# Two junctions of a two-block transformer kernel: second output projection reordered, gate/up token sums made from PSUM

## The reference

```python
mixed = jnp.concatenate([rms_norm_2(attn, attn_out_norm[l]),
                         rms_norm_2(sgu, sgu_out_norm[l])], axis=-1)
y = mixed @ w_out[l]                                   # second output projection
x = x + rms_norm_2(y, post_mix_norm[l])
h = rms_norm_2(x, pre_ffn_norm[l])
f = (jax.nn.silu(h @ w_gate[l]) * (h @ w_up[l])) @ w_down[l]
x = x + rms_norm_2(f, post_ffn_norm[l])
```

## Time and profile before

| | |
|---|---|
| median of 3 runs | 2080.42 us (2078.24 to 2081.92) |
| the profiled execution | 2081.29 us, its span 2079.5 us |
| TensorE busy | 2004.0 us, 96% of the span, 10021 matmuls |
| VectorE, ScalarE, GpSimd busy | 1325.6, 846.2, 960.3 us (64%, 41%, 46%) |
| mean granted TensorE clock | 0.987 of full speed |
| chain that ended last | TensorE 79%, VectorE 11%, ScalarE 5%, GpSimd 2% |

### The profile page before, as it was taken

The page is one execution under the profiler, slowest core; times in us unless marked ns, Lnnn a source line. Parts: engine busy times, 40 slices in busy tenths (PEclk is TensorE's granted clock), DMA queues, the critical chain, the costliest instruction groups (busy, mean ns, idle before and its releaser), DMA issues.

```text
span 2079.5 us, 27399 instructions
## 1 busy us (share of the span) xinstructions
PE 2004.0 (96%) x10021; PEld 1662.3 (80%) x10021; DVE 1325.6 (64%) x1744; ACT 846.2 (41%) x1349; POOL 960.3 (46%) x564
## 2 busy tenths in 40 slices
PE   7999999999999999999999899897999999999997
PEld 6888888888887778878887689775788888878885
DVE  7887777756637655874331543799665656657977
ACT  5444544434420034560202676566333332334443
POOL 1344555332233477733542200848755555435552
PEclk8999999999999999999999999999999999999998
DMA  9223212211122143242111000231333323346344
GB/s 282 69 81 112 100 53 95 85 30 41 41 62 62 61 172 112 102 142 63 50 40 59 23 1 1 71 116 58 120 107 106 111 90 102 120 171 229 101 140 150
DMA packets 178925, 193.98 MB, mean 93 GB/s; under 512 B 9799, under 2 KB 122904, under 8 KB 178842
## 3 DMA queue, kind: packets, MB, share of 16 engines
q1 hardware_dynamic: 172420, 178.53, 26.9%
q10 hardware_dynamic: 6422, 14.37, 1.9%
HBM read 151.71 MB, written 41.16 MB: 93 GB/s over the span
## 4 chain that ended last, share of the span: by engine, by line
PE 79%; DVE 11%; ACT 5%; issue 3%; POOL 2%; ACTq 0%; DMA 0%; SPq 0%; DVEq 0%; POOLq 0%
PE psum L994 6%; PE psum L996 6%; PE psum L995 6%; PE psum L1533 6%; PE psum L1534 6%; PE psum L1535 6%; PE psum L1155 3%; PE psum L1632 3%; PE psum L1634 3%; PE psum L1633 3%; PE psum L1015 3%; PE psum L1016 3%; PE psum L1014 3%; PE psum L1436 3%; PE psum L1310 2%
## 5 line engine op out<-in xcount | busy, mean ns | idle before, releaser
L777 POOL TENSOR_TENSOR w_hi<-w_raw,ones 128x1024 fp32r<-128x1024 f32 x60 | 149.3, 2489 | 480.9 <-PE psum L996 356.7
L994 PE MATMUL psum<-h_hi,w_hi 128*128 128x512 f32 x704 | 284.1, 404 | 0.0
L996 PE MATMUL psum<-h_hi,w_lo 128*128 128x512 f32 x704 | 274.7, 390 | 0.0
L995 PE MATMUL psum<-h_lo,w_hi 128*128 128x512 f32 x704 | 274.2, 390 | 0.0
L1664 ACT ACTIVATE arena<-psum 128x1024 f32<-128x1024 f32 (+7 forms) x134 | 100.3, 752 | 215.6 <-PE psum L996 134.0
L780 POOL TENSOR_TENSOR w_lo<-w_raw,w_hi 128x1024 fp32r<-128x1024 f32 x60 | 167.9, 2799 | 4.7
L995 PEld LDWEIGHTS psum<-h_lo,w_hi 128*128 128x128 f32 x704 | 132.4, 188 | 28.4 <-issue 2.6
L994 PEld LDWEIGHTS psum<-h_hi,w_hi 128*128 128x128 f32 x704 | 132.3, 188 | 28.4 <-issue 2.6
L996 PEld LDWEIGHTS psum<-h_hi,w_lo 128*128 128x128 f32 x704 | 132.1, 188 | 28.5
L1632 PE MATMUL psum<-w_hi,h_hi 128*128 128x512 f32 x308 | 122.0, 396 | 8.1 <-DVE h_lo L3220 5.1
L1633 PE MATMUL psum<-w_lo,h_hi 128*128 128x512 f32 x308 | 121.5, 394 | 0.0
(11 more groups left out here) (483 smaller groups left out, 5315.6 us busy)
## 6 DMA issues: line engine op xcount, KB each, us to landing
w_raw<-w_in SPq DMA_DIRECT2D x64, 512.0 KB, 3.8
act_op<-arena SPq DMA_DIRECT2D x77, 256.0 KB, 2.2
arena<-act_op SPq DMA_DIRECT2D x77, 256.0 KB, 2.7
w_raw<-w_gate SPq DMA_DIRECT2D x22, 512.0 KB, 4.0
w_raw<-w_up SPq DMA_DIRECT2D x22, 512.0 KB, 5.1
arena<-ada_w SPq DMA_DIRECT2D x16, 512.0 KB, 7.2
arena<-w_out SPq DMA_DIRECT2D x16, 512.0 KB, 6.0
out_T<-arena SPq DMA_DIRECT2D x16, 512.0 KB, 5.6
```

What stands on the lines that cost most here:

```text
L994: pe.matmul(o, wh, xh, start=(k == 0), stop=False)
L995: pe.matmul(o, wh, xl, start=False, stop=False)
L996: return pe.matmul(o, wl, xh, start=False, stop=(k == KT - 1))
```

## The change

**In the projection.** GpSimd makes S1 right behind the low parts of P7 (n == 7) and T4 behind those of n == 11. VectorE takes the last attention block (`attended`) after the first low part of P1, normalises before the last one, and lays copies 1 and 3 between the low parts of steps 4 to 7; the four S2 sums come behind step 7's. ScalarE loads the table for Sqrt before its last attention copies, rounds P7's right operands before the norm, and makes copies 0 and 2 inside the loop, behind the roundings for n = 5 and n = 7; the high parts of steps 4 to 7 wait for step 0 alone. TensorE does transposes 2 and 3 one tile earlier in step 3.

**At the junction.** ScalarE makes `r12` only, three passes for each strip. VectorE makes T1, T3 and T2 of a strip as scalar-tensor-tensor operations that read B12 or B22 from PSUM. T3 is now B22 - B12, and S3 is A11 - A21 for every pair, so that their product is unchanged. All 16 low parts of the T sums are made by VectorE. GpSimd makes `whole` 0 to 3 ahead of pair 1's weight sums, then only weights. TensorE transposes the first three token tiles of B12 and B22 before the fourth is normalised (now by ScalarE), does transposes k + 2 behind the products of strip k, and the order of pair 1 is A11, A12, S4, S1, S3, S2, A22. ScalarE's table load, Silu and roundings lie between the strips.

```diff
-SECOND_PRODUCTS = ["A11", "A12", "S4", "S2", "S1", "S3", "A22"]
+SECOND_PRODUCTS = ["A11", "A12", "S4", "S1", "S3", "S2", "A22"]
...
                 if n == 7:
                     for i in range(QJ):
+                        q_sum("S1", i)
+                if n == 11:
+                    for i in range(QJ):
                         q_sum("T4", i)
-                    for i in range(QJ):
-                        q_sum("S1", i)
...
-            t_lo(0, "T2", t2_raw)
-            t_lo(1, "T1", r11)
+            second_lo("S1")
+            second_lo("S3")
             second_lo("S2")
-            second_lo("S1")
-            t_lo(2, "T3", r22)
-            second_lo("S3")
             second_lo("A22")
-            t_lo(3, "T4", r21)
...
-                        if (n, t) == (3, 3):
+                        if (n, t) == (3, 2):
                             pe.wait_ge(*raw_ready(0))
                             q_transpose(2)
...
             pe.wait_ge(o_sums, Q_C0 + Q_C11[3])
+            pe.wait_ge(xn_done, 3 * NT - 1)
+            b_transpose(0, range(3))
+            b_transpose(1, range(3))
             pe.wait_ge(xn_done, 3 * NT)
-            b_transpose(0)
-            b_transpose(1)
+            b_transpose(0, [3])
+            b_transpose(1, [3])
...
-                    act.wait_ge(o_step, Q_STEP + n - 3)
+                    act.wait_ge(o_step, Q_STEP + (n - 3 if n >= 8 else 1))
...
-            for j in range(QJ):
-                q_hi_b(QJ + j, "P7", j)
-            q_raw_copy(0)
-            q_raw_copy(2)
             for n in Q_ORDER_A[4:]:
                 q_hi_a(n, O_PRODUCTS[n // QJ], n % QJ)
                 if n < 24:
                     q_hi_b(n + 4, O_PRODUCTS[n // QJ + 1], n % QJ)
+                if n in (5, 7):
+                    q_raw_copy(n - 5)
...
-            q_raw_copy(1)
-            q_raw_copy(3)
+            q_lo(3, "P1", 3)
             dve.wait_ge(row_in, 48)
             for n in Q_ORDER_A[4:]:
                 q_lo(n, O_PRODUCTS[n // QJ], n % QJ)
-                if 4 <= n < 8:
-                    q_s2(n - 4)
+                if n in (4, 6):
+                    q_raw_copy(n // 2 * 2 - 3)
+                if n == 7:
+                    for j in range(QJ):
+                        q_s2(j)
...
+                STT(r11[:, k, :], b12, mul(k), r11[:, k, :], ALU.mult, ALU.subtract).then_inc(t_sum, 1)
+                STT(r22[:, k, :], b22_, mul(k + 4), r12[:, k, :], ALU.mult, ALU.subtract).then_inc(t_sum, 1)
+                dve.wait_ge(t_sum, 3 * k + 1)
+                STT(t2_raw[:, k, :], b22_, mul(k + 4), r11[:, k, :], ALU.mult, ALU.subtract).then_inc(t_sum, 1)
...
+            t_lo("T1", r11, lambda k: 3 * k + 3)
+            t_lo("T3", r22, lambda k: 3 * k + 3)
             dve.wait_ge(gp_done, NPR)
             dve.wait_ge(silu_b_done, 1)
             TT(act_lo, psum[:, P_BANK["u2"], :], u2_of[0], ALU.mult).then_inc(act_b_done, 1)
-            for k in range(2, 4):
-                dve.wait_ge(t_sum, 2 * k + 2)
+            dve.wait_ge(s0_done, S0_BASE + KT)
+            for k in range(4):
                 TT(r21[:, k, :], t2_raw[:, k, :], r21[:, k, :], ALU.subtract).then_inc(t_sum, 1)
+            t_lo("T2", t2_raw, lambda k: 3 * k + 3)
+            t_lo("T4", r21, lambda k: 12 + k + 1)
```

More of the change, by code:

```diff
@@ L937, in _ @@
             TT(s_raw["S4"], A12, s_raw["S2"], ALU.subtract).then_inc(s_done_w, 1)
[L938 to L957 removed]
+            TT(s_raw["S3"], A11, A21, ALU.subtract).then_inc(s_done_w, 1)
             for name in ("A11", "A12", "S4"):
@@ L2111, in _ @@
                 if n == N - 1:
+                    A(lb_tmp, ones[:, 0:8], ACT.Sqrt)
                     q_raw_copy(4)
@@ L2117, in _ @@
                 q_hi_a(j, "P1", j)
-            A(lb_tmp, ones[:, 0:8], ACT.Sqrt)
+            for j in range(QJ):
+                q_hi_b(QJ + j, "P7", j)
             act.wait_ge(ao_done, 2 * NT)
@@ L2209, in _, with b_taken, t_hi @@
             q_root(5)
-            for name in ("A11", "A12", "S4"):
-                second_hi(name)
+            second_hi("A11")
+            q_xn(5, 3, 2)
             act.wait_ge(spilled_a, 16 * 4)
             act.wait_ge(spilled_b, 16 * 2)
-            for k in range(4):
+            def b_taken(k):
                 act.wait_ge(tr_full, T_BASE[4] + KT + 2 * k + 2)
-                for e, (name, raw) in enumerate((("B12", r12), ("B22", r22))):
+                for e, name in enumerate(("B12", "B22")):
                     src = psum[:, 4 + (2 * k + e) % 4, :]
                     A(x_hi[name][:, k, :], src, ACT.Identity, scale=mul(k + 4 * e)).then_inc(b22_taken, 1)
-                    A(raw[:, k, :], src, ACT.Identity, scale=mul(k + 4 * e)).then_inc(b22_taken, 1)
+                    if name == "B12":
+                        A(r12[:, k, :], src, ACT.Identity, scale=mul(k)).then_inc(b22_taken, 1)
+            def t_hi(k):
+                for a, (name, raw) in enumerate((("T1", r11), ("T3", r22), ("T2", t2_raw))):
+                    act.wait_ge(t_sum, 3 * k + a + 1)
+                    copy(x_hi[name][:, k, :], raw[:, k, :]).then_inc(t_rounded, 1)
+            b_taken(0)
+            b_taken(1)
+            second_hi("A12")
             act.wait_ge(gp_done, 1)
             A(silu_of[0], psum[:, P_BANK["g1"], :], ACT.Silu).then_inc(silu_a_done, 1)
-            for a, name, raw in ((2, "T2", t2_raw), (1, "T1", r11)):
-                for k in range(4):
-                    act.wait_ge(t_sum, 2 * k + a)
-                    copy(x_hi[name][:, k, :], raw[:, k, :]).then_inc(t_rounded, 1)
+            second_hi("S4")
+            b_taken(2)
+            t_hi(0)
+            b_taken(3)
+            for k in range(1, 4):
+                t_hi(k)
             act.wait_ge(spilled[1], 16 * 2)
@@ L2229, in _ @@
             act.wait_ge(gp_done, NPR)
-            second_hi("S2")
-            second_hi("S1")
-            for k in range(4):
-                act.wait_ge(t_sum, 8 + k + 1)
-                copy(x_hi["T3"][:, k, :], r22[:, k, :]).then_inc(t_rounded, 1)
-            second_hi("S3")
-            second_hi("A22")
+            for name in ("S1", "S3", "S2", "A22"):
+                second_hi(name)
             for k in range(4):
@@ L2293, in _ @@
             each = [[name] for name in PRODUCTS]
-            gu_pair(1, 1, SECOND_PRODUCTS, [["A11"], [], [], ["S2"], ["S1"], ["S3"], ["A22", "A12", "S4"]], False)
+            gu_pair(1, 1, SECOND_PRODUCTS, [["A11"], [], [], [], [], ["S2", "S1", "S3"], ["A22", "A12", "S4"]], False)
             with act.Fori(1, FT // 2 - 1) as j:
@@ L3009, in _ @@
             q_raw_copy(7)
-            for j in range(QJ):
+            q_lo(0, "P1", 0)
+            attended(2 * NT - 1)
+            for j in range(1, 3):
                 q_lo(j, "P1", j)
-            attended(2 * NT - 1)
             def q_s2(j):
@@ L3194, in sum_next @@
                 x, y, op = {"S1": (A21, A22, ALU.add), "S2": (s_raw["S1"], A11, ALU.subtract),
-                            "S3": (A21, A11, ALU.subtract), "S4": (A12, s_raw["S2"], ALU.subtract)}[name]
+                            "S3": (A11, A21, ALU.subtract), "S4": (A12, s_raw["S2"], ALU.subtract)}[name]
                 TT(s_raw[name], x, y, op).then_inc(s_done_w, 1)
```

66 lines of the change are left out of this document (32 added, 34 removed).

## The result

The changed kernel takes 2067.57 us (median of 6 runs, 2064.41 to 2069.29), the kernel before 2081.06 (6 runs, 2078.24 to 2084.95): ratio 0.9933, 95% interval 0.9922 to 0.9943, a gain of 13.5 us where 20.4 were forecast. The profiled execution took 2067.42 us (span 2065.4), against 2081.29 (2079.5) before.

What follows compares the result with a forecast made beforehand. TensorE, busy 96% of the span, was taken as the bound, so only its waits and clock could give time. Gains of 7.8 and 12.6 made 20.4 us: 2060.0 on the median, stated as 2061, range 2057 to 2068.

Steps and rivals of the forecast that it cites:

- rival 3: Projection: the wait only moves, another operand holding steps 8 and 9 for 4 to 5 us; 2066 us, chance 0.05.
- First part: Output projection steps 3 to 7: reordered GpSimd, VectorE and ScalarE work shortens TensorE's waits, gain 7.8 us.
- the 0.89 us wait in front of the transposes: Projection, after steps 0 to 2: TensorE's wait there disappears and the transposes start at 1311.9.
- A wait of about 2.1 us replaces the one of 2.30: Projection, before step 4: TensorE waits until 1320.3 for ScalarE's copy, then steps 4 and 5 run through.
- Steps 6 to 11 have their low parts in time: Projection: VectorE's S2 sums end near 1328, step 8's low part at 1329.6, and step 8 starts at 1331.3.
- Second part: Junction from 1416 to the end of pair 1: PSUM-fed sums, earlier transposes and moved low parts gain 12.6 us.
- First plain product 1421.0: Junction, first strip: TensorE starts its first plain product at 1421.0, after VectorE's second low part ends at 1420.7.
- End of pair 1, 1453.2: Junction: TensorE ends the first gate/up pair at 1453.2, against 1466.1 before.
- rival 1: Clock: idling about 3.0 us before the first strip brings half-clock matmuls costing 1.2 to 2.6 us; 2063 to 2066, chance 0.22.
- Outside both places the change leaves TensorE's stream alone: Rest of the kernel, beyond projection and junction: TensorE's stream is unchanged, so gains stay to the end.
- Rival 2: Junction, 1443 to 1452: VectorE late by its own low parts beside GpSimd, TensorE stands some 11 us; 2071.5, chance 0.08.
- Rival 4: Pairs 1 to 3: VectorE becomes the bound, PSUM-fed sums also at 1.67 us, 24.9 us late; 2084.5, chance 0.03.

Runs made afterwards that it cites:

- e1: Only the projection's edits, junction as in the kernel before: 2078.26 us against 2081.36 before, ratio 0.9985.
- e3: The changed kernel with one wait more: GpSimd begins P7's low parts only when VectorE's normalisations are done; 2063.19 us, ratio 0.9911.
- e4: e3 with ScalarE's copy 2 put ahead of the rounding that waits for step 3: 2063.05 us, ratio 0.991.
- e6: The changed kernel with sums T1, T2, T3 read from SBUF and ScalarE making B22's scaled copy too: 2072.12 us, ratio 0.9955.
- e7: e4 with all four of product 3's first sums made by VectorE after low part 17: 2066.09 us, ratio 0.9927.
- e2: Only the junction's edits, projection as in the kernel before: 2071.44 us, ratio 0.9941.
- e5: The changed kernel with the sixteen low parts of the four token sums given back to GpSimd: 2076.4 us, ratio 0.9977.
- e8: The changed kernel once more, unaltered, for its profile alone: 2066.36 us.

## Why the prediction was right and where it failed

The direction, the range (2057 to 2068) and most of the mechanism held; the point, 2061, was 6.6 us too low. Most of that is in the first part, in two steps: one wait that was put at nothing, and VectorE's queue behind it. That rival 3's value, 2066, lies near the measured one is luck.

- **First part, forecast 7.8, measured 2.8 in the profile and 3.1 alone (e1). This is the step that failed.** The prediction said: "ScalarE's four scalings (2.56 us) end near 1310.9, before TensorE is through. So the 0.89 us wait in front of the transposes goes". It counted ScalarE's half of the normalisation and left out VectorE's four (1.68 us in before's trace at 1310.10, shorter than ScalarE's as long as GpSimd is idle), and it did not ask what GpSimd would be doing. The moved rounding started GpSimd earlier, and its low parts ran beside VectorE's operations: 5.25 us and not 1.68. The wait was 2.97 us where none was forecast. e3 takes this one cause away: 2.0 us in the projection's stretch, 4.4 by the medians. The statistics' 1.1 us stayed in e3, where the 128 x 8 operation (1308.58) took 1.26. The Trainium skill has the rule (SBUF — State Buffer, Who interferes with whom): copy, cast and tensor_scalar can enter a mode that takes the ports that VectorE shares with GpSimd, when their operands meet its conditions, and then one of the two engines blocks; an operation with a single SBUF input is free of GpSimd only outside that mode. The trace agrees, with 1.3 us for an operation that issues every 0.4 us alone. The prediction priced GpSimd's presence only for operations with two SBUF inputs.
- **"A wait of about 2.1 us replaces the one of 2.30".** It was 1.72, released by ScalarE's copy as said, and none at step 5. Right. e4 adds that the copy's place in ScalarE's queue is worth little: with it out of the way VectorE's copy ends the wait 0.5 us earlier.
- **"Steps 6 to 11 have their low parts in time".** They had. But the prediction took it that nothing behind them is short of time, and there VectorE is late: its output sums come 2.2 to 2.3 us late in e1, e3, e4 and e6, and a stop taken away ahead of them (e3), or there (e7), comes back in part or whole. So 7.8 was not to be had by the first part as written, even without the slow normalisations: with them mended the stretch gives 92.13 - 87.37 = 4.8 us (e3), and the other 3.0 lie behind, with that wait and its half clock.
- **Second part, forecast 12.6, measured 11.5 to the end of pair 1, and 11.4 there alone (e2; 9.9 by the medians).** PSUM-fed sums at 0.66 a piece: right (0.74 busy, starts 0.66 apart), and e6 puts 4.5 us on them and on the pass that ScalarE is spared. First plain product 1421.0: counted from the closing transposes, as before's clock has them, it was 1420.27 + 1395.61 - 1394.99 = 1420.9. No wait of TensorE in pair 1: right. The low parts moved to VectorE are worth 8.8 us (e5). End of pair 1, 1453.2: on that clock 1454.7, late by the 1.6 us of half clock behind the 2.81 us wait. That is rival 1, in part, and it was the rule and not the exception: in the seven profiles with this wait at 2.81 us (the changed kernel, e2, e3, e4, e5, e7, e8) six to eight matmuls at half clock follow in six, and none in e3 alone. The sum should have carried it. Inside the part two errors met: T3's low parts were forecast at 1.67 us each beside GpSimd and took 0.61, T4's sums were forecast at 0.75 and took 1.57. That the operands came in time rests on the two together.
- **Outside.** "Outside both places the change leaves TensorE's stream alone, so a gain made here stays to the end": true of the stream, but 2.15 us were lost upstream and 1.6 won at the down projection, by waits and clock that differ from one execution to another.

Rival 2 (VectorE late by its low parts) did not come: T4's sums ran beside GpSimd at 1.57 each, T2's and T4's low parts at 0.62 and 0.90 (3.58 us for T4's four). Rival 3 did not come: steps 8 and 9 have no wait of 4 to 5 us. Rival 4 is excluded by the PSUM-fed sums' 0.74.

## What to carry to other kernels

When an edit makes an engine start earlier, list what ran on the other engines in the gap that it used to leave, and price each of those again as if it ran beside it: here GpSimd's idle 4.1 us was what kept four VectorE operations at 0.4 us each. One wait that gives that gap back won 2.0 us in the projection and 4.4 by the medians, beside 2.8 and 3.1 for the whole reordering it belongs to. And where the waits of the fast engine change from one execution to the next while the stretch keeps its length, look at the queue of another engine before pricing any one wait: e7 took a 2.32 us wait away and got one of 3.94.

## What the runs showed of the hardware

- A VectorE operation with one SBUF input and a scalar column is slowed beside GpSimd as those with two inputs are: 1.68 us for four alone, 5.25 beside it. A 128 x 8 one took 1.25 us and not 0.17, so a tiny operation lost 1.1 us, most of one of GpSimd's 128 x 512 sums (6.37 us for four). The PSUM-fed sums took 0.74 us both beside GpSimd (1420.04) and with it idle (1432.00).
- It is not always VectorE that pays. VectorE's eight low parts in a row (1434.64) kept 0.61 us each, and GpSimd's operation beside them took 3.71 us; T4's four sums right behind (1440.05) took 1.57 each, and GpSimd's beside them 1.74.
- The granted clock after a wait of a given length is not the same from one execution to another. Behind the same 2.81 us wait at the junction eight matmuls ran at half clock in the changed kernel, six to eight in five other profiles, and none in e3 (granted clock 1.00). At the down projection 2.97 us was followed by six slow ones before; 2.57 by none after, nor was 3.06 us in e8. The four waits of 3.9 us agree better: thirteen followed each of 3.91 and 3.92 us before and 3.92 in e1, twelve that of 3.94 in e7. An estimate of a wait's price should carry 0 to 1.6 us for it at 2 to 3 us, and some 2.6 at 3.9.
